# Two stacked transformer programs on one core: the first block's first weight piece in five parts, squares moved, latent tiles ahead of the query squares, and turned tiles between the gates

## The reference, cut to what matters

```python
xn = rms_norm(h, norm_gain)
q_a, k_a, v_a, g_a, q_i, k_i, w_i, c_q, c_kv, k_rope, g_b = split(xn @ w_in)
# heads a: per-head norm, rope; each query keeps 128 keys picked by an indexer
score = sum_h w_i[h] * relu(q_i[h] . k_i)         # o_a = attention over the top 128 of score
# heads b: queries and keys are expanded from normalised latents
q_b = rms_norm(c_q) @ w_uq                        # 8 heads of 96
k_nope, v_b = split(rms_norm(c_kv) @ w_ukv)       # 8 heads of 64 + 64
q_b, k_b = per-head rms_norm and rope             # o_b = block-causal attention
h = h + concat(o_a * silu(g_a), o_b * silu(g_b)) @ w_out
```

## Time and profile before

| | us |
|---|---|
| median of the three timed runs | 2730.4 |
| lowest, highest | 2729.37, 2731.22 |
| the profiled execution, device time | 2733.43 |
| its span on the core | 2731.6 |

### The profile page before, as it was taken

The page is one execution under the profiler, slowest core; times in us unless marked ns, Lnnn a source line. Parts: engine busy times, 40 slices in busy tenths (PEclk is TensorE's granted clock), DMA queues, the critical chain, the costliest instruction groups (busy, mean ns, idle before and its releaser), DMA issues.

```text
span 2731.6 us, 32035 instructions
## 1 busy us (share of the span) xinstructions
PE 2664.5 (98%) x12868; PEld 2130.4 (78%) x12868; DVE 1467.1 (54%) x2603; ACT 1120.0 (41%) x1509; POOL 1185.1 (43%) x896
## 2 busy tenths in 40 slices
PE   8998999999999999999999999999999999999997
PEld 7786677778888877768888876788888777788886
DVE  5797555557554135667554145475532565575522
ACT  4534634444333236553333235443333344443331
POOL 3353443235445532245445541354455332454453
PEclk9899999999999999999999999999999999999999
DMA  4125032222223321112223231222233222222232
GB/s 162 62 102 176 1 116 85 78 78 93 93 94 110 106 96 62 62 62 93 94 107 108 104 113 47 73 98 93 93 110 117 97 86 70 93 93 93 100 116 77
DMA packets 45605, 253.44 MB, mean 93 GB/s; under 512 B 4560, under 2 KB 9184, under 8 KB 17936
## 3 DMA queue, kind: packets, MB, share of 16 engines
q1 hardware_dynamic: 34656, 232.18, 24.0%
q10 hardware_dynamic: 10800, 19.20, 2.2%
HBM read 249.21 MB, written 10.55 MB: 95 GB/s over the span
## 4 chain that ended last, share of the span: by engine, by line
PE 88%; DVE 4%; ACT 3%; POOL 2%; issue 1%; DMA 1%; DVEq 0%; SPq 0%; ACTq 0%
PE ring L454 74%; PE ring L869 3%; POOL wlo L1085 2%; PE turn L874 2%; PE turn L454 1%; PE out L913 1%; DMA raw<-in_pieces 1%; PE ring L706 1%; PE ring L607 1%; ACT whi L1134 1%; PE out L722 1%; PE out L957 1%; DVE sp L2034 1%; PE out L919 0%; DVE e L2002 0%
## 5 line engine op out<-in xcount | busy, mean ns | idle before, releaser
L1085 POOL TENSOR_TENSOR wlo<-raw,whi 128x512 fp32r<-128x512 f32 x860 | 1150.8, 1370 | 1464.8 <-ACT whi L1134 1464.7
L454 PE MATMUL ring<-xh,whi 128*128 128x512 f32 x1888 | 753.3, 399 | 12.0 <-DVE xl L1585 8.2
L454 PE MATMUL ring<-xh,wlo 128*128 128x512 f32 x1888 | 736.5, 390 | 0.0
L454 PE MATMUL ring<-xl,whi 128*128 128x512 f32 x1888 | 736.2, 390 | 0.0
L1134 ACT ACTIVATE whi<-raw 128x2048 fp32r<-128x2048 f32 x215 | 411.6, 1915 | 426.3 <-DMA raw<-in_pieces 411.1
L454 PEld LDWEIGHTS ring<-xh,whi 128*128 128x128 f32 x1888 | 355.0, 188 | 117.4 <-issue 44.0
L454 PEld LDWEIGHTS ring<-xh,wlo 128*128 128x128 f32 x1888 | 354.8, 188 | 75.3
L454 PEld LDWEIGHTS ring<-xl,whi 128*128 128x128 f32 x1888 | 355.3, 188 | 72.6 <-issue 3.4
L2141 DVE SCALAR_TENSOR_TENSOR taps<-u,conv,taps 128x511 f32<-128x511 f32 (+1 forms) x344 | 294.6, 901 | 18.2 <-ACT taps L1528 14.9
L2155 DVE TENSOR_TENSOR u<-ring,r 128x512 f32<-128x512 f32 x168 | 114.5, 687 | 300.2 <-PE ring L454 300.2
L2131 DVE TENSOR_TENSOR h<-ring,h 128x512 f32<-128x512 f32 x72 | 49.6, 689 | 415.3 <-PE ring L795 376.7
(11 more groups left out here) (281 smaller groups left out, 3371.9 us busy)
## 6 DMA issues: line engine op xcount, KB each, us to landing
raw<-in_pieces SPq DMA_DIRECT2D x215, 1024.0 KB, 4.7
toep<-diag_store ACTq DMA_DIRECT2D x16, 512.0 KB, 3.6
diag_store<-diag_row ACTq DMA_DIRECT2D x1, 5120.0 KB, 27.7
band_store<-band_row ACTq DMA_DIRECT2D x1, 3072.0 KB, 34.5
h<-in_x SPq DMA_DIRECT2D x4, 512.0 KB, 6.7
wbias<-band_store ACTq DMA_DIRECT2D x4, 512.0 KB, 7.4
result<-h SPq DMA_DIRECT2D x8, 256.0 KB, 2.1
raw<-in_pieces SPq DMA_DIRECT2D x4, 256.0 KB, 6.8
```

Of the source, the lines that this page charges most:

```text
L454: ins = pe.matmul(out, stationary, moving, start=first and n == 0, stop=last and n == 2)
L1085: ins = pool.tensor_tensor(m.wlo[slot][:, part], m.raw[slot][:, part], m.whi[slot][:, part].bitcast(F32), ALU.subtract)
```

## The change

1. The first piece and x land in five parts of 1, 1, 2, 2 and 2 tiles (`FIRST_PARTS`), which makes two DMAs more. The squares are put off: those of k = 0 and 1 stand behind the third part, 2 and 3 behind the fourth, and 4 to 7 behind the split of piece 1.
2. `bias_diagonals` waits for the three constants that it reads (`hot_landed`), and no longer for all nine.
3. ACT's squares of q_b move from the end of `expand_q` to behind the latent tiles of `latents_kv`. PE begins `expand_kv` with the first tile's part of units 0 and 1 as soon as that tile is there, and adds the second tile's part after it.
4. The four turned tiles of pair 0 move out of `attn` into `gates`, one after each of gate units 1 to 4, on PE and on DVE.
5. After the first scores DVE takes the tiles of pair 1 before it makes the mask and normalises; the mask was made before the scores.

```diff
 def pair_units():
-    order = [("prep", 0, *u) for u in pair_preps(0)] + [("gate", 6), ("gate", 7)]
+    order = [("gate", 6), ("gate", 7)]
...
+GATES = [("gate", 0)]
+for u in range(1, 6):
+    GATES += [("gate", u)] + [("prep", 0, *x) for x in pair_preps(0)[u - 1:u]]
...
+FIRST_PARTS = ((0, 1), (1, 2), (2, 4), (4, 6), (6, 8))
+
+SQUARED_AFTER = ((), (), (0, 1), (2, 3), (), (4, 5, 6, 7))
...
         square_sum(st["norm_in"])
-        pe.wait_ge(m["consts"], N_CONSTS)
+        pe.wait_ge(m["hot_landed"], 3 * 16)
         bias_diagonals(b)
...
     def expand_kv(b):
+        def unit(n, tiles, **parts):
+            expand_unit(b, n, 0, n // 2, 512 * (n % 2), 512, 1024, tiles, **parts)
         wait_piece(b, 0)
+        pe.wait_ge(m["ct_hi"], 8)
+        pe.wait_ge(m["unit_taken"], b.at("unit_taken", -1))
+        for n in range(2):
+            unit(n, [(0, 0)], last=False)
         pe.wait_ge(m["ct_hi"], 10)
         pe.wait_ge(m["unit_taken"], b.at("unit_taken", 0))
         pe.wait_ge(m["ix_taken"], INDEX_TURNS + 2 * INDEX_PAIRS)
         sums = latent_sums(m.out, (0, 1))
-        for n in range(KV_UNITS):
-            expand_unit(b, n, 0, n // 2, 512 * (n % 2), 512, 1024, [(0, 0), (1, 1)], sums)
+        for n in range(2):
+            unit(n, [(1, 1)], sums=sums, first=False)
+        for n in range(2, KV_UNITS):
+            unit(n, [(0, 0), (1, 1)], sums=sums)
...
+    def gates(b):
+        for n, unit in enumerate(GATES):
+            if unit[0] == "gate":
+                gate(b, n, *divmod(unit[1], 2))
+            else:
+                pe.wait_ge(m["qkb_ready"], 1)
+                wait_unit_free(b, n)
+                turn_heads(m.ring[b.slot("unit_ready", n, 4)], *unit[1:])
...
     def first(b):
         act.preload_act_table_set("natural_log_exp_and_others")
         act.wait_ge(m["gain_landed"], 16)
...
+        for q, (lo, hi) in enumerate(FIRST_PARTS):
+            part = slice(256 * lo, 256 * hi)
+            act.wait_ge(m[f"first_landed{q}"], 16)
+            act.activation(m.whi[0][:, part], m.raw[0][:, part], ACT.Copy).then_inc(m["first_hi"], 1)
+            act.wait_ge(m[f"x_landed{q}"], 16)
+            for k in range(lo, hi):
+                split_x(b, k, C_NORM0)
+            for k in SQUARED_AFTER[q]:
+                square(b, k)
+        split_hi(b, 1)
+        for k in SQUARED_AFTER[-1]:
             square(b, k)
-        split_hi(b, 1)
...
         latent_tile(b, 0, 0)
         latent_tile(b, 1, 1)
+        act.wait_ge(m["unit_taken"], b.at("unit_taken", 0))
+        act.wait_ge(m["acced"], 2 * INDEX_PAIRS)
+        square_heads(m.sq_b[1], m.q_b)
         small_rsqrt("q_b")
         small_rsqrt("kv_latent")
...
-        act.wait_ge(m["unit_taken"], b.at("unit_taken", UQ_UNITS))
-        act.wait_ge(m["acced"], 2 * INDEX_PAIRS)
-        square_heads(m.sq_b[1], m.q_b)
...
-        take_prep(0)
         pick_round(14)
         take_gate(b, UNITS[("gate", 6)], 6)
         pick_round(15)
         take_gate(b, UNITS[("gate", 7)], 7)
-        make_mask()
         dve.wait_ge(m["gate_ready"], 8)
         for s in range(PAIRS + 3):
             if s < PAIRS:
                 scores(s)
             if s >= 3:
                 low(s - 3)
+            if s == 0:
+
+                take_prep(1)
+                make_mask()
             if s < PAIRS:
                 take_reciprocal(s, 0)
                 normalise(s)
-            if s + 1 < PAIRS:
+            if 1 <= s < PAIRS - 1:
                 take_prep(s + 1)
```

More of the change, by code:

```diff
@@ L250, in piece_ends @@
                 ends.append(("unit_ready", b.at("unit_ready", (2, 4, 8)[j])))
+            elif name == "gates":
+                ends.append(("unit_ready", b.at("unit_ready", GATE_UNITS[("gate", 2 * j + 1)] + 1)))
             elif name == "attn":
@@ L547, in index_q @@
         for k in range(KT):
-            pe.wait_ge(m["first_lo"], k // 2 + 1)
+            pe.wait_ge(m["first_lo"], [lo <= k < hi for lo, hi in FIRST_PARTS].index(True) + 1)
             pe.wait_ge(m["xl_ready"], k + 1)
@@ L595, in latent_sums, with expand_unit @@
                 yield
-    def expand_unit(b, n, j, t, lo, cols, width, tiles, sums):
-        wait_unit_free(b, n)
+    def expand_unit(b, n, j, t, lo, cols, width, tiles, sums=iter(()), first=True, last=True):
+        if first:
+            wait_unit_free(b, n)
         slot, tok = b.slot("piece", j, SLOTS), slice(t * P, (t + 1) * P)
@@ L606, in expand_unit @@
             for x, weights in passes:
-                ins = pe.matmul(out, x[:, tok], weights[slot][:, w], start=i == 0 and weights is m.whi and x is passes[0][0],
-                                stop=i == len(tiles) - 1 and x is m.ct_l[tile])
-                if not (i == len(tiles) - 1 and x is m.ct_l[tile]):
+                begins = first and i == 0 and weights is m.whi and x is passes[0][0]
+                ends = last and i == len(tiles) - 1 and x is m.ct_l[tile]
+                ins = pe.matmul(out, x[:, tok], weights[slot][:, w], start=begins, stop=ends)
+                if not ends:
                     next(sums, None)
                     next(sums, None)
-        ins.then_inc(m["unit_ready"], 1)
+        if last:
+            ins.then_inc(m["unit_ready"], 1)
     def heads(b):
@@ L675, in expand_kv, with turn_heads, gate @@
         sums = latent_sums(m.out, (0, 1))
-        for n in range(KV_UNITS):
-            expand_unit(b, n, 0, n // 2, 512 * (n % 2), 512, 1024, [(0, 0), (1, 1)], sums)
+        for n in range(2):
+            unit(n, [(1, 1)], sums=sums, first=False)
+        for n in range(2, KV_UNITS):
+            unit(n, [(0, 0), (1, 1)], sums=sums)
+    def turn_heads(out, p, x, j):
+        rows = B_QK if p < PAIRS_B else P
+        for t in range(TT):
+            if p < PAIRS_B:
+                src = (m.q_b if x == "q" else m.k_b)[:, 2 * p + j, t, :]
+            else:
+                src = (m.q_a if x == "q" else m.k_a)[:, t, p - PAIRS_B, :]
+            ins = pe.transpose(out[0:rows, t * P:(t + 1) * P], src, m.ident[:])
+        ins.then_inc(m["unit_ready"], 1)
+    def gate(b, unit, j, half):
+        if half == 0:
+            wait_piece(b, j)
+        wait_unit_free(b, unit)
+        for k in range(KT):
+            ins = feature_group(b.slot("piece", j, SLOTS), half, k, X[k], m.ring[b.slot("unit_ready", unit, 4)][:])
+        ins.then_inc(m["unit_ready"], 1)
+    def gates(b):
+        for n, unit in enumerate(GATES):
+            if unit[0] == "gate":
+                gate(b, n, *divmod(unit[1], 2))
+            else:
+                pe.wait_ge(m["qkb_ready"], 1)
+                wait_unit_free(b, n)
+                turn_heads(m.ring[b.slot("unit_ready", n, 4)], *unit[1:])
     def attn(b, ob):
@@ L724, in pv @@
             ins.then_inc(m["pv_done"], 1)
-        pe.wait_ge(m["qkb_ready"], 1)
-        prep(0)
-        wait_piece(b, 0)
         for half in range(2):
-            out = bank(("gate", 6 + half))
-            for k in range(KT):
-                ins = feature_group(b.slot("piece", 0, SLOTS), half, k, X[k], out[:])
-            ins.then_inc(m["unit_ready"], 1)
+            gate(b, UNITS[("gate", 6 + half)], 0, half)
         for s in range(PAIRS + 2):
@@ L1036, in tensor_program @@
         elif name == "gates":
-            for j in range(3):
-                feature_piece(b, j, X)
+            gates(b)
         elif name == "index_q":
@@ L1295, in gates @@
                 split_hi(b, 2 + u // 2)
-            silu(b, u, u)
+            silu(b, GATE_UNITS[("gate", u)], u)
     def heads(b):
```

88 lines of the change are left out of this document (41 added, 47 removed).

## The result

| | median us | lowest to highest |
|---|---|---|
| before, 16 runs | 2729.48 | 2725.51 to 2731.22 |
| changed, 16 runs | 2734.52 | 2729.56 to 2737.98 |

The ratio is 1.0019, 95% interval 1.0012 to 1.0025. The changed kernel is about 5 us slower; 2717.5 was forecast. Its profiled execution took 2733.4 us, and the one of before 2733.43, some 4 us above before's own median. So the two traces look equal at the end, although the kernels are not.

What follows compares the result with a forecast made beforehand. PE, busy 98% of the span, was taken as the bound, leaving its idle time and low-clock matmuls to win. Terms of 1.5 + 5.7 + 5.7 = 12.9 us off the 2730.4 median gave 2717.5, range 2713.5 to 2724.

Steps and rivals of the forecast that it cites:

- Term 1: Start: PE begins piece 1 at 23.1 in place of 24.64, a gain of 1.5 us.
- I let ACT wait for it about 1.2 us: Start: ACT's allowed wait for the later-issued third part, with piece 1's split then starting near 15.7 us.
- Rival B: Start bound by bytes: halves land as late as before, term 1 is nothing, 2719.0 us; chance 0.14.
- The last addition ends about 3.3 us after the split: Start: DVE's additions of the squares end at 20.8 us, so the sum of squares stays at 20.8 to 21.8.
- Term 2: Latents: the wait for `ct_l` mostly goes, units 4 to 7 of `expand_kv` end earlier, a gain of 5.7 us.
- rival A: `expand_kv`: the clock falls at the new wait, 24 matmuls at 1.2 GHz take 4.8 us more, 2722.3; chance 0.14.
- the ring: Four banks between PE and DVE: DVE, moving up about 5 us, may take gate unit 0 by PE's fifth unit's start.
- Term 3: Gates and first pairs: `qp` wait goes and pair 1's takes come sooner, a gain of 5.7 us.
- Its second part: Term 3 in the pairs, from the first scores on: a further gain of 2.4 us.
- Its first part: Term 3 in the gates: first scores start at 237.5 in place of 240.83, 3.3 us.
- rival C: Pairs: term 3's second half is given back to their steady chain, 3.3 in place of 5.7, 2719.9; chance 0.09.
- Rival D: Gates: ACT's DMA issue delays gate units 6 and 7; slower than before above 21.2 us; chance 0.04 with other losses.

Runs made afterwards that it cites:

- e1: Changed kernel with the old start restored (four parts, each square behind its tile), keeping the bias table's own wait: 2726.49 us, ratio 0.9988 to before.
- e5: Changed kernel with all eight squares ahead of the split of piece 1 again, five parts kept: 2732.89 us, ratio 1.0014 to before.
- e11: Changed kernel with four equal parts, squares 4 to 7 still put off, POOL's low part of piece 1 waiting for DVE's additions: 2730.56 us, ratio 0.9997 to before.
- e3: Kernel before with the latents' part alone (q_b's squares moved, expand_kv begun with the first tile): 2732.39 us, ratio 1.0011 to before.
- e8: e1 with two of DVE's pick rounds moved from ahead of q_a's head sums into the gates: 2725.79 us, ratio 0.9991 to before.
- e12: e10 with pick round 2 also moved behind k_b's head sums: 2723.48 us, ratio 0.9975 to before.
- e14: e1 with two pick rounds moved in halves into the pairs, the mask behind them: 2725.35 us, ratio 0.9983 to before.
- e4: Kernel before with gates and pairs alone (turned tiles among the gates, pair 1's takes ahead of the mask): 2722.07 us, ratio 0.9973 to before.
- e2: Kernel before with the new start alone (five parts, squares put off, bias table's own wait): 2736.26 us, ratio 1.003 to before.
- e7: e1 with POOL's six low parts in heads left out, ACT copying the high part instead, so not the reference's result: 2719.94 us, ratio 0.9967 to before.
- e10: e1 with pick rounds 5 and 6 moved beside round 4, ahead of k_a's norm: 2724.44 us, ratio 0.9977 to before.
- e13: e4 with the pick-round moves of e12, as a control: 2723.70 us, ratio 0.9974 to before.
- e16: e4 run once more, beside e14 on the same chip: 2723.70 us, ratio 0.9979 to before.

## Why the prediction was wrong, step by step

**Term 1 (1.5 us gained; 6.6 lost in the trace, 8.0 by e1).** Two steps failed.

- "I let ACT wait for it about 1.2 us" for the third part. ACT waited 1.8 us for the second and 2.5 for the third, 4.3 in all, for an earlier first part that gave back 1.6; e5 shows 2.6 us of delay from the parts alone. I priced the smaller first part and the later issue of one part, but put the wait for the second part at nothing and did not reckon with slower bytes, which the rates show. Rival B had the place right; its price, nothing at worst, was too small. My lower bound of zero had no row behind it.
- "The last addition ends about 3.3 us after the split", at 20.8. It ended at 27.0. I costed the additions at 0.69 us each, although the edit put them beside POOL's low part of piece 1, and took no account of that. e11 restores 0.69 us and the order of times that I had in mind.

**Term 2 (5.7 us).** Its own sum was right: 5.9 us in the changed kernel, 5.95 in e3. (The working is loose by 0.2 us: 111.1 and the 2.1 us behind it give 113.2 for the first take, not 113.4.) Inside it, two things traded places. The first wait was 1.3 us for the 0.7 forecast. Behind it the clock either stayed at 1.00, and PE waited 1.3 us for ACT's take (e5, e8, e11, e12, e14) where 2.6 were forecast, or it fell for some 3 us, and there was no wait: 0.76 over 110 to 117 us in the changed kernel and 0.76 over 104 to 111 in e1 and e3, which stand some 6 us earlier. The latent stages took 26.8 to 26.9 us either way. So rival A's clock did come in some executions, but it used up the wait for ACT and cost nothing. What failed is the sentence behind it, "DVE moves up a little less than PE, which the ring covers". DVE did not move up at all: it was 7.9 us later with q_a than before, and 1.4 later in e1, which has the old start, while PE reached `heads` 8.9 us earlier there. POOL's low parts came in bunches, and beside the turns of k_a and q_a, which doubled what it costs DVE (11.6 to 23.5 us in e1). In the changed kernel the ring also covered less than I said, because term 3 put prep units of 0.5 us into it: the fifth unit now comes after three gate units and one prep (16.8 us), not after four (21.8). e3, without these units, lost as much, so that is not the main cause. The price was in the trace of before: the same 128x1024 operation on the same line stood there at 1.22 and at 2.31 us, the long ones beside POOL's low parts (L1659 at 165.51 and at 191.43). I had read no view of DVE in heads, as it was off PE's path.

**Term 3 (5.7 us).** Right in the sum, as e4 shows: 2.9 + 2.5 = 5.4 us in the trace. Its second part was there in the changed kernel too (2.4). Its first part was hidden there by the late gate units. But the second part is measured from a trace with a low clock behind the 3.1 us wait. Counted from the first scores, the second pair's come at 7.96 in e4 for 9.50, and the third pair's at 18.30 for 20.59 in before but for 18.91 in e2, whose clock stayed at 1.00. So of the 1.5 us gained at the second pair 0.6 are left at the third: rival C held for the pairs by themselves, and the rest of the 2.4 was that a wait and its low clock stayed away. That my number fits is partly luck of before's profiled execution. Rival D didn't come: DVE waited 0.7 us for the last silu itself, as counted, and not for ACT's issue ahead of it.

**The slower rival** was the wrong one. Mine (ACT's issue) needed 21 us of issue. The real mechanisms were two losses of 5 to 8 us. That of the start rests on late bytes and on DVE beside POOL, that of the heads on DVE beside POOL alone. The chance of 0.04 came from looking only for delays on the engines that the change touches, never at POOL, which it doesn't touch.

## What to carry to other kernels

Before moving work of an engine, list what will run beside it on the other engines at its new time, and look in the trace for the same instruction at two durations: that row shows the price of an overlap. A gain of PE in front of a stage is worth only the margin of the engine that is last behind that stage, so its chain must be followed to the next place where PE waits for it. And a change of several parts should be timed part by part: here one part was worth more alone than the whole.

## What the runs showed of the hardware that was not expected

- VectorE operations with two SBUF inputs beside GpSimd's subtraction: 128x512 from 0.69 to 1.6 to 1.8 us, 128x1024 from 1.22 to 2.3, 128x2048 from 2.29 to 3.3, 128x32 from 0.19 to 1.21. GpSimd's own eight went from 10.1 to 18.0 us.
- The first weights in parts of 128, 128 and three times 256 KB, each with twice as many bytes of x: 283 to 342 GB/s over 6 to 9 us in three kernels, against 351 to 386 in thirteen with four parts of 256 KB. The 256 KB part behind the two small ones was ready for ACT 7.3 us after its issue (3.52 to 10.79).
- The same instructions from piece 1 to `latents_kv` took 65.0 us in e1 and e3 and 68.0 in before and e7, which all have the old start. The granted clock over 24 to 30 us was 1.00 in the first two and 0.72 in the others, and over 70 to 75 us 1.00 against 0.71 and 0.69. PE had idled 0.3 us right ahead of piece 1 in e1 and e3, and 1.6 us in front of it in before and e7. In e4, e8, e10, e13 and e16, with 0.6 to 1.4 us, the stretch took 66.5. A single profiled execution of this kernel carries 3 us of that.
